# Prompt heads of a decoder step in pairs: scores from two row halves, values into two column halves

## The chip, the cores and the metric

The kernel runs on one core of a Trainium2 chip. A core has a matrix engine (TensorE, PE in the profile; PEld is its loading of weights), VectorE (DVE), ScalarE (ACT), GpSimd (POOL) and SyncE (SP), which work side by side and tell each other of progress through semaphores. Transfers between the chip's main memory and the on-chip memory are issued by SP and POOL and carried out by DMA engines. TensorE writes to PSUM, eight banks of 128 partitions x 512 floats, and VectorE and ScalarE read it from there. The metric is the time of one execution on the device in microseconds (us), lower is better.

## What is computed

One layer of a decoder for 256 prompt tokens and 64 sample tokens (8 sequences of 8), 2048 wide, all in float32: RMS norm, one projection whose columns are shared by three groups (a gated MLP, windowed attention with 16 heads of 64, cross-attention into 256 memory tokens with 4 heads of 128), an output projection, and a mixture of experts. The change concerns the windowed attention of the prompt:

```python
def dilated_attend_prompt(q, k, v, rel_bias):
    ...
    for window, dil in DILATIONS:
        ...
        sc = jnp.einsum("brnqhe,brnkhe->brnhqk", qs, kk) * scale + bias
        sc = jnp.where(valid[None, None, :, None], sc, -jnp.inf)
        m = jnp.max(sc, axis=-1, keepdims=True)
        p = jnp.exp(sc - m)
        l = jnp.sum(p, axis=-1, keepdims=True)
        o = jnp.einsum("brnhqk,brnkhe->brnqhe", p / l, vv)
        ...
    return combine_by_denominator(outs, lses).astype(dtype)
```

The three patterns, mixed by their softmax denominators, are one softmax per query over all keys, in which a key counts as often as patterns reach it. The kernel puts that count, as a logarithm, into the bias.

## The kernel before

The order of the work on each engine is written out by hand: all engines walk through the same 108 steps of the input projection. A step `s` does one unit on TensorE (`unit`): four 128-row slices of the model's width times 512 columns for one group of tokens. Units with `s % 3` of 0 and 1 have 128 tokens and fill the whole array (L499, 4 products). The third has the 64 sample tokens and puts two products of 256 columns into two column halves of the array (L502, 8 products). The weights come through a ring of four buffers that SP refills, four units of three steps ahead.

Attention is fitted between the units. Tables of step numbers say when:

- `START` holds the first step of each of eight sample units `n` (two sequences each). In steps 0 to 2 of a unit its keys are multiplied (`qk`, L613, L619), VectorE adds the bias (`soften`, L1139 to L1151), ScalarE takes the exponential (`sample_exp`, L930), in steps 3 to 5 the weights are transposed (`turn_s`, L629), in steps 4 to 6 they meet the values (`pv`, L646), and one step later the parts are folded (`fold`, L653).
- `HEAD_AT` holds one step for each of 16 prompt heads `h` (38 to 45, 74 to 81) and 4 memory heads (92 to 95). In that step TensorE makes the head's scores from the 64 rows of its half (`scores`, L556, L557, PSUM bank 3), VectorE adds the bias and takes the maximum (`head_max`, L1090 to L1097), and ScalarE the exponential (`head_exp`, L919, L920). One step later VectorE divides (`head_share`, L1103 to L1105), TensorE turns the three blocks of weights (`turn_p`, L570 to L572, bank 4) and ScalarE copies them back (`head_turned`, L926). Two steps later TensorE multiplies them with the values (`head_values`, L591, L592, bank 5, the 64 partitions of the head's half), and after each second head VectorE copies the pair out (`head_out`, L1112). The weights live in three buffers, `sc_p[h % 3]`.
- `NORM_AT` and `TURN_AT` place the norms of queries and keys on VectorE (`squares_of`, `normalise`, L1055 to L1077) and their transposes (L540, L542). Before each sample unit VectorE fills its padded query (`pad_q`, L1121).

Within a step TensorE does the unit first, then the scores, then sample work, then values and turns of heads.

Of the kernel before, what the change touches and what calls it, by code (L numbers as in the profile page):

```python
# [24 lines left out]
ALU = mybir.AluOpType  # L25
# [11 lines left out]
H, DH = 16, 64  # L37
HP = H // 2
G, DG = 4, 128
# [71 lines left out]
def hybrid_step(nc, x_rows, mem_rows, x_t, mem_t, w_proj, w_o, kc, vc, mkc, mvc, cst_d, gv_d, gffn_d,  # L111
                relb_d, onehot_d, w_gu, w_dn, mst_d, o_y, o_k, o_v, o_va, o_mk, o_mv,
                bias_d, bias_q_d):
    with ExitStack() as ctx:
# [374 lines left out]
        def _(pe):  # L489
# [55 lines left out]
            def scores(h):  # L545
                if h == 0:
                    pe.wait_ge(tr_used, 12)
                if h == 8:
                    pe.wait_ge(tr_used, 20)
                if h == H:  # L550
                    pe.wait_ge(tr_used, 24)
                if h:
                    pe.wait_ge(sc_read, h)
                if h < H:
                    r, hp = slice(64 * (h % 2), 64 * (h % 2) + 64), h % 8 // 2
                    mm(ps[:, 3, 0:128], qT[r, hp, 0:128], kT[r, hp, 0:128], start=True, stop=True)  # L556
                    mm(ps[:, 3, 128:384], qT[r, hp, 128:256], kT[r, hp, 0:256], start=True, stop=True).then_inc(sc_mm, 1)  # L557
                else:
                    g = h - H
                    mm(ps[:, 3, 0:256], qmT[:, g, 0:128], mkT[:, g, :], start=True, stop=True)  # L560
                    mm(ps[:, 3, 256:512], qmT[:, g, 128:256], mkT[:, g, :], start=True, stop=True).then_inc(sc_mm, 1)

            def turn_p(h):

                pe.wait_ge(p_ready, h + 1)
                if h:
                    pe.wait_ge(pt_ready, h)
                p = sc_p[h % 3]
                if h < H:
                    mm(ps[:, 4, 0:128], p[:, 0:128], c("flip"), start=True, stop=True)  # L570
                    mm(ps[:, 4, 128:256], p[:, 128:256], c("flip"), start=True, stop=True)
                    mm(ps[:, 4, 256:384], p[:, 256:384], c("flip"), start=True, stop=True).then_inc(pt_mm, 1)  # L572
                else:
                    tr(ps[:, 4, 0:128], p[:, 0:128], ident)
                    tr(ps[:, 4, 128:256], p[:, 256:384], ident)
                    tr(ps[:, 4, 256:384], p[:, 128:256], ident)
                    tr(ps[:, 4, 384:512], p[:, 384:512], ident).then_inc(pt_mm, 1)

            def head_values(h):
                pe.wait_ge(pt_ready, h + 1)  # L580
                pt = sc_p[h % 3]
                if h < H:
                    r = slice(64 * (h % 2), 64 * (h % 2) + 64)
                    if h == 0:
                        pe.wait_ge(z_ready, 4 + 9)
                    if h == 8:
                        pe.wait_ge(z_ready, 4 + 18)
                    if h % 2 == 0 and h >= 2:
                        pe.wait_ge(y_used, h // 2)
                    v = [z[:, Z_V[h // 8], t, (h % 8) * DH:(h % 8 + 1) * DH] for t in range(2)]  # L590
                    mm(ps[r, 5, 0:256], v[0], pt[:, 0:256], start=True, stop=False, skip_group_check=True)  # L591
                    mm(ps[r, 5, 128:256], v[1], pt[:, 256:384], start=False, stop=True, skip_group_check=True).then_inc(pv_mm, 1)  # L592
                else:
                    g = h - H
                    pe.wait_ge(y_used, HP + g)
                    mm(ps[:, 5, 0:256], mv[:, 0, g * DG:(g + 1) * DG], pt[:, 0:256], start=True, stop=False)
                    mm(ps[:, 5, 0:256], mv[:, 1, g * DG:(g + 1) * DG], pt[:, 256:512], start=False, stop=True).then_inc(pv_mm, 1)
# [115 lines left out]
            for s in range(UNITS_X):  # L713
# [154 lines left out]
        def _(act):  # L868
# [45 lines left out]
            def head_exp(h):  # L914
                act.wait_ge(mx_ready, h + 1)
                b, w0, w = h % 3, *((128, 384) if h < H else (256, 512))
# [97 lines left out]
        def _(dve):  # L1014
# [92 lines left out]
            def head_out(h):  # L1107
                if h < H and h % 2 == 0:
                    return
# [456 lines left out]
```

## Time and profile before

| | |
|---|---|
| median of 3 runs | 1237.83 us (1234.96 to 1239.39) |
| the profiled execution | 1238.09 us, span 1236.2 us |
| TensorE busy | 1125.1 us (91%) |
| VectorE, ScalarE, GpSimd busy | 349.5, 219.9, 39.9 us |
| mean share of the DMA engines | 76.1% for the main queue |
| the chain that ended last | TensorE 73%, DMA 19%, VectorE 3% |

The span is the time from the first to the last instruction. The chain is followed back from the last instruction, at each step to what released it. Projection and attention come first in the span, then the output projection, the routing and the loop over experts. A row of the timeline gives a start, a length, and in brackets how long the engine was idle before and for whom. Matmuls overlap at their ends, so what a group of them costs is read from its start to the start of the next.

### The profile page before, as it was taken

To read this page: it belongs to the slowest core of one execution; us is meant where nothing else is said; L and a number is where in the kernel's file an instruction comes from. 1 tells how busy PE (TensorE), PEld (TensorE's weight loads), DVE (VectorE), ACT (ScalarE), POOL (GpSimd) and SP (SyncE) were. 2 spreads that over 40 slices of the span, in tenths; PEclk is the share of its full clock that TensorE was granted. 3 is DMA by queue.
4 is the path that set the end of the run, shared out by engine and by line. 5 is a ranking of instruction groups with operands and counts; after the bars stand their busy time and mean duration, and the time that the engine had idled before them with its cause. 6 is when DMAs were issued, how large, how long until landed. Compare 5 with 4: busy or idle time off the path is not lost.

```text
span 1236.2 us, 15447 instructions
## 1 busy us (share of the span) xinstructions
PE 1125.1 (91%) x6547; PEld 480.1 (39%) x6547; DVE 349.5 (28%) x702; ACT 219.9 (18%) x434; POOL 39.9 (3%) x38
## 2 busy tenths in 40 slices
PE   6999999998999999999999995997979797979786
PEld 2344444553444554554444442232323232222222
DVE  2131112332211433250001114242424242333333
ACT  0400102220111221430001013121212211111120
POOL 0111010010010000010000000000000000000000
PEclk9999999999999999999999997998989898989899
DMA  7997246778999878752683213999999999999993
GB/s 246 361 354 302 103 142 261 276 302 324 380 337 366 337 284 317 318 217 102 256 344 118 85 34 137 426 433 429 432 424 432 430 434 428 435 429 426 435 426 142
DMA packets 33194, 385.20 MB, mean 312 GB/s; under 512 B 4207, under 2 KB 6383, under 8 KB 8655
## 3 DMA queue, kind: packets, MB, share of 16 engines
q1 hardware_dynamic: 31584, 378.96, 76.1%
q0 software_dynamic: 1568, 5.62, 1.5%
q8 instruction: 33, 0.54, 0.2%
q14 instruction: 9, 0.07, 0.0%
HBM read 376.67 MB, written 7.90 MB: 311 GB/s over the span
## 4 chain that ended last, share of the span: by engine, by line
PE 73%; DMA 19%; DVE 3%; ACT 2%; issue 2%; SPq 1%; POOL 1%; ACTq 0%; DVEq 0%; POOLq 0%
PE ps L499 27%; DMA arena<-w_gu 14%; PE ps L832 8%; PE ps L502 7%; PE ps L857 5%; PE ps L817 4%; PE ps L646 3%; DMA arena<-w_proj 3%; PE ps L613 3%; PE ps L844 3%; PE ps L837 1%; PE ps L862 1%; PE ps L629 1%; DMA arena<-x_rows 1%; PE ps L542 1%
## 5 line engine op out<-in xcount | busy, mean ns | idle before, releaser
L499 PE MATMUL ps<-arena 128*128 128x512 f32 x960 | 435.2, 602 | 12.5 <-DMA arena<-w_proj 12.5
L499 PEld LDWEIGHTS ps<-arena 128*128 128x128 f32 x960 | 176.7, 191 | 221.7 <-issue 220.1
L832 PE MATMUL ps<-arena 128*32 128x512 f32 x1024 | 133.0, 666 | 41.1 <-DMA arena<-w_gu 40.1
L817 PE MATMUL ps<-arena 128*32 128x512 f32 (+1 forms) x792 | 97.6, 606 | 6.5 <-DVE arena L1340 6.5
L502 PE MATMUL ps<-arena 128*64 128x256 f32 x832 | 101.3, 385 | 0.0
L832 PEld LDWEIGHTS ps<-arena 128*32 128x32 f32 x1024 | 35.8, 121 | 137.5 <-issue 122.4
L844 PE MATMUL ps<-arena 128*32 128x512 f32 x512 | 67.1, 645 | 20.6 <-DVE arena L1363 20.6
L1361 DVE STREAM_TRANSPOSE arena<-ps 128x512 f32<-128x512 f32 x32 | 22.9, 717 | 208.2 <-PE ps L817 208.2
L502 PEld LDWEIGHTS ps<-arena 128*64 128x64 f32 x832 | 55.1, 136 | 47.3 <-issue 23.5
L857 PE MATMUL ps<-arena 128*128 128x512 f32 x128 | 57.0, 598 | 9.5 <-ACT arena L1010 9.5
L1378 DVE COPY arena<-ps 32x512 f32<-32x512 f32 x64 | 44.2, 691 | 49.3 <-PE ps L844 48.3
L1003 ACT COPY arena<-ps 128x512 f32<-128x512 f32 x32 | 18.8, 586 | 205.4 <-PE ps L832 205.4
L817 PEld LDWEIGHTS ps<-arena 128*32 128x32 f32 (+1 forms) x792 | 23.0, 109 | 74.3 <-issue 74.3
L1008 ACT COPY arena<-ps 32x512 f32<-32x512 f32 x64 | 36.8, 575 | 82.1 <-PE ps L844 81.3
L1383 DVE TENSOR_TENSOR arena<-ps,arena 128x512 f32<-128x512 f32 x64 | 44.2, 691 | 21.3 <-PE ps L857 21.3
L1263 DVE TENSOR_TENSOR arena<-ps,arena 128x512 f32<-128x512 f32 (+1 forms) x16 | 8.9, 556 | 127.8 <-PE ps L499 122.9
L646 PE MATMUL ps<-arena 128*32 128x256 f32 (+1 forms) x704 | 44.0, 383 | 0.0
L1404 POOL TENSOR_TENSOR stat<-stat,nhalf 128x24 f32<-128x24 f32 (+4 forms) x9 | 25.0, 2781 | 564.5 <-DVE stat L1057 365.7
L613 PE MATMUL ps<-arena 128*32 128x512 f32 (+1 forms) x384 | 40.5, 540 | 2.9 <-issue 2.9
L837 PEld LDWEIGHTS ps<-arena 128*128 128x128 f32 x256 | 31.0, 191 | 26.8 <-issue 26.8
L857 PEld LDWEIGHTS ps<-arena 128*128 128x128 f32 x128 | 23.7, 190 | 37.3 <-issue 26.8
L898 ACT ACTIVATE arena<-ps,stat 128x512 f32<-128x512 f32 (+1 forms) x36 | 20.8, 578 | 95.7 <-PE ps L499 85.0
(226 smaller groups left out, 757.3 us busy)
## 6 DMA issues: line engine op xcount, KB each, us to landing
arena<-w_gu SPq DMA_DIRECT2D x32, 4096.0 KB, 21.8
arena<-w_dn SPq DMA_DIRECT2D x32, 2048.0 KB, 20.3
arena<-w_proj SPq DMA_DIRECT2D x44, 1024.0 KB, 7.3
arena<-kc SPq DMA_DIRECT2D x16, 2048.0 KB, 8.5
arena<-vc SPq DMA_DIRECT2D x16, 2048.0 KB, 8.6
arena<-w_o SPq DMA_DIRECT2D x16, 1024.0 KB, 4.8
arena<-kc SPq DMA_DIRECT2D x8, 1024.0 KB, 8.5
arena<-vc SPq DMA_DIRECT2D x8, 1024.0 KB, 9.0
```

The source lines that it names most:

```text
L499: last = mm(ps[:, bank + t, :], src[:, kt, r0:r0 + m], wring[:, i % QTR, k, :], start=start, stop=stop)
L502: last = mm(ps[64 * j:64 * j + 64, bank + t, 0:256], src[:, kt, r0:r0 + m], wring[:, i % QTR, k, 256 * j:256 * j + 256], start=start, stop ...
L613: last = mm(ps[32 * g:32 * g + 32, 6, 0:w], qpad[:, e * 128 + 32 * g:e * 128 + 32 * g + 32], kp[j][:, e, :], start=half == 0, stop=half == 1)
L646: last = mm(ps[32 * g:32 * g + 32, 7, 0:256], pt_s[0:w, t, 32 * g:32 * g + 32], v, start=t == 0, stop=t == VT)
L817: last = mm(ps[32 * j:32 * j + 32, 1, :], pm[0:m, t, 32 * s:32 * s + 32], n2[0:m, t, 512 * j:512 * j + 512], start=t == 0, stop=t == 2)
L832: last = mm(ps[g:g + 32, 0, :], xgT[:, r, kt, :], wgu[r][:, kt, :], start=kt < 4, stop=kt >= KT - 4)
L837: last = mm(ps[:, 2, 32 * f:32 * f + 32], part[:, 128 * f:128 * f + 128], sel, start=True, stop=True)
L844: last = mm(ps[32 * g:32 * g + 32, 3, :], actT[:, j, :], wdn[r][:, j, 512 * g:512 * g + 512], start=j == 0, stop=j == 1)
L857: mm(ps[:, 4 + n, :], pwT[:, t * P:(t + 1) * P], y4[:, 512 * n:512 * n + 512], start=True, stop=True).then_inc(comb_mm, 1)
L1008: copy(y4[32 * s:32 * s + 32, 512 * g:512 * g + 512], ps[32 * g:32 * g + 32, 3, :]).then_inc(ye_copied, 1)
L1378: V.tensor_copy(y4[32 * s:32 * s + 32, 512 * g:512 * g + 512], ps[32 * g:32 * g + 32, 3, :]).then_inc(ye_copied, 1)
L1383: V.tensor_tensor(hh, ps[:, 4 + n, :], hh, ALU.add).then_inc(added[t], 1)
```

## The change

The 16 prompt heads are handled as eight pairs, at the steps of `PAIR_AT`. A pair's scores are made in one go in the first step: the two heads lie in rows 0 to 63 and 64 to 127, their products alternate, and they go to banks 3 and 4. VectorE and ScalarE take maximum and exponential of both heads in that step and divide in the next. Two steps after the scores TensorE turns all six blocks, back into banks 3 and 4, and ScalarE copies both. Three steps after the scores, which is the step of the next pair's scores, the values of both heads are multiplied, alternating between the two column halves, into bank 5. Weights now live in `sc_p[0]` and `sc_p[1]`. Memory heads keep their functions, steps and order under new names.

```diff
-HEAD_AT = [38 + h for h in range(8)] + [74 + h for h in range(8)] + [92 + g for g in range(4)]
+PAIR_AT = (38, 41, 44, 47, 74, 77, 80, 83)
...
+def place(h):
+
+    return (h % 2, 128, 384) if h < H else ((h - H) % 3, 256, 512)
...
+            def pair_scores(p):
+
+                pe.wait_ge(tr_used, 12 if p < 4 else 20)
+                if p:
+                    pe.wait_ge(pt_ready, 2 * p)
+                hp = p % 4
+                lo, hi = slice(0, 64), slice(64, 128)
+                mm(ps[:, 3, 0:128], qT[lo, hp, 0:128], kT[lo, hp, 0:128], start=True, stop=True)
+                mm(ps[:, 4, 0:128], qT[hi, hp, 0:128], kT[hi, hp, 0:128], start=True, stop=True)
+                mm(ps[:, 3, 128:384], qT[lo, hp, 128:256], kT[lo, hp, 0:256], start=True, stop=True).then_inc(sc_mm, 1)
+                mm(ps[:, 4, 128:384], qT[hi, hp, 128:256], kT[hi, hp, 0:256], start=True, stop=True).then_inc(sc_mm, 1)
+
+            def pair_turn(p):
+
+                pe.wait_ge(sc_read, 2 * p + 2)
+                for k in range(2):
+                    pe.wait_ge(p_ready, 2 * p + k + 1)
+                    for a in range(0, 384, 128):
+                        last = mm(ps[:, 3 + k, a:a + 128], sc_p[k][:, a:a + 128], c("flip"), start=True, stop=True)
+                    last.then_inc(pt_mm, 1)
+
...
+            def pair_values(p):
+
+                pe.wait_ge(pt_ready, 2 * p + 2)
...
+                if p:
+                    pe.wait_ge(y_used, p)
+
+                def v(k, t):
+                    h = 2 * (p % 4) + k
+                    return z[:, Z_V[p // 4], t, h * DH:(h + 1) * DH]
+                lo, hi = slice(0, 64), slice(64, 128)
+                mm(ps[lo, 5, 0:256], v(0, 0), sc_p[0][:, 0:256], start=True, stop=False, skip_group_check=True)
+                mm(ps[hi, 5, 0:256], v(1, 0), sc_p[1][:, 0:256], start=True, stop=False, skip_group_check=True)
+                mm(ps[lo, 5, 128:256], v(0, 1), sc_p[0][:, 256:384], start=False, stop=True, skip_group_check=True)
+                mm(ps[hi, 5, 128:256], v(1, 1), sc_p[1][:, 256:384], start=False, stop=True, skip_group_check=True).then_inc(pv_mm, 1)
...
-                for h in range(H + G):
-                    if s == HEAD_AT[h]:
-                        scores(h)
+                for p, at in enumerate(PAIR_AT):
+                    if s == at + 3:
+                        pair_values(p)
+                for p, at in enumerate(PAIR_AT):
+                    if s == at:
+                        pair_scores(p)
...
-                for h in range(H + G):
-                    if s == HEAD_AT[h] + 2:
-                        head_values(h)
-                for h in range(H + G):
-                    if s == HEAD_AT[h] + 1:
-                        turn_p(h)
...
+                for p, at in enumerate(PAIR_AT):
+                    if s == at + 2:
+                        pair_turn(p)
...
             def head_turned(h):
                 w = 384 if h < H else 512
                 act.wait_ge(pt_mm, h + 1)
-                copy(sc_p[h % 3][:, 0:w], ps[:, 4, 0:w]).then_inc(pt_ready, 1)
+                copy(sc_p[place(h)[0]][:, 0:w], ps[:, 3 + h % 2 if h < H else 4, 0:w]).then_inc(pt_ready, 1)
...
-                for h in range(H + G):
-                    if s == HEAD_AT[h]:
-                        head_exp(h)
+                for p, at in enumerate(PAIR_AT):
+                    if s == at:
+                        head_exp(2 * p)
+                        head_exp(2 * p + 1)
...
-                for h in range(H + G):
-                    if s == HEAD_AT[h] + 1:
-                        head_turned(h)
+                for p, at in enumerate(PAIR_AT):
+                    if s == at + 2:
+                        head_turned(2 * p)
+                        head_turned(2 * p + 1)
...
-                    V.scalar_tensor_tensor(sc_p[b][:, 0:128], ps[:, 3, 0:128], S_WIN, bias[:, 128:256], ALU.mult, ALU.add)
-                    last = V.scalar_tensor_tensor(sc_p[b][:, 128:384], ps[:, 3, 128:384], S_WIN, bias, ALU.mult, ALU.add)
+                    V.scalar_tensor_tensor(sc_p[b][:, 0:128], ps[:, 3 + b, 0:128], S_WIN, bias[:, 128:256], ALU.mult, ALU.add)
+                    last = V.scalar_tensor_tensor(sc_p[b][:, 128:384], ps[:, 3 + b, 128:384], S_WIN, bias, ALU.mult, ALU.add)
...
-                for h in range(H + G):
-                    if s == HEAD_AT[h] + 1:
-                        head_share(h)
+                for p, at in enumerate(PAIR_AT):
+                    if s == at + 1:
+                        head_share(2 * p)
+                        head_share(2 * p + 1)
...
-                for h in range(H + G):
-                    if s == HEAD_AT[h]:
-                        head_max(h)
+                for p, at in enumerate(PAIR_AT):
+                    if s == at:
+                        head_max(2 * p)
+                        head_max(2 * p + 1)
...
-                for h in range(H + G):
-                    if s == HEAD_AT[h] + 2:
-                        head_out(h)
+                for p, at in enumerate(PAIR_AT):
+                    if s == at + 3:
+                        head_out(p)
```

On TensorE, in steps 40 and 41, before: L646 are sample values, L629 sample transposes, L591 and L592 a head's values, L570 to L572 its turns, L502 the third unit, L556 and L557 the next head's scores.

```order
L646 MATMUL ps<-arena 32x256 x16
L629 MATMUL ps<-cst,arena 128x128 x4
L591 MATMUL ps<-arena 64x256
L592 MATMUL ps<-arena 64x128
L570 MATMUL ps<-cst,arena 128x128
L571 MATMUL ps<-cst,arena 128x128
L572 MATMUL ps<-cst,arena 128x128
L502 MATMUL ps<-arena 64x256 x8
L556 MATMUL ps<-arena 128x128
L557 MATMUL ps<-arena 128x256
```

The same place now, where L663 are sample values, L646 sample transposes, L569 the six turns of pair 0, L508 the third unit, L584 to L587 the values of pair 0 and L558 to L561 the scores of pair 1:

```order
L663 MATMUL ps<-arena 32x256 x16
L646 MATMUL ps<-cst,arena 128x128 x4
L569 MATMUL ps<-cst,arena 128x128 x6
L508 MATMUL ps<-arena 64x256 x8
L584 MATMUL ps<-arena 64x256
L585 MATMUL ps<-arena 64x256
L586 MATMUL ps<-arena 64x128
L587 MATMUL ps<-arena 64x128
L558 MATMUL ps<-arena 128x128
L559 MATMUL ps<-arena 128x128
L560 MATMUL ps<-arena 128x256
L561 MATMUL ps<-arena 128x256
```

The turns stand next to the sample transposes, the values next to the third unit, which has their shape, and the scores of the next pair follow them.

On TensorE, in steps 49 and 50, before, there is no head work: L499 is the unit of step 49, L646 are the last sample values of unit 1, L502 is the unit of step 50, L613 the first sample scores of unit 2.

```order
L499 MATMUL ps<-arena 128x512 x4
L646 MATMUL ps<-arena 32x256 x12
L502 MATMUL ps<-arena 64x256 x8
L613 MATMUL ps<-arena 32x512 x8
L653 MATMUL ps<-cst,arena 128x32 x2
```

Now the turns (L569) and the values (L584 to L587) of pair 3 stand between these sample values (L663) and the sample scores (L630):

```order
L505 MATMUL ps<-arena 128x512 x4
L663 MATMUL ps<-arena 32x256 x12
L569 MATMUL ps<-cst,arena 128x128 x6
L508 MATMUL ps<-arena 64x256 x8
L584 MATMUL ps<-arena 64x256
L585 MATMUL ps<-arena 64x256
L586 MATMUL ps<-arena 64x128
L587 MATMUL ps<-arena 64x128
L630 MATMUL ps<-arena 32x512 x8
```

The work of the pair's end moved past the end of sample unit 1.

On VectorE, in step 38, before: a head's bias and maximum (L1090 to L1097) and then the last part of the scores of sample unit 0 (L1142, L1146) and its maximum (L1151).

```order
L1090 SCALAR_TENSOR_TENSOR arena<-ps,arena 128x128
L1091 SCALAR_TENSOR_TENSOR arena<-ps,arena 128x256
L1096 TENSOR_REDUCE stat<-arena 128x1
L1097 TENSOR_REDUCE stat<-arena 128x1
L1142 SCALAR_TENSOR_TENSOR arena<-ps,arena 128x256
L1146 SCALAR_TENSOR_TENSOR arena<-ps,arena 64x64 x2
L1151 TENSOR_REDUCE stat<-arena 128x1
```

Now the same for two heads (L1123 to L1130 twice) and then the sample unit (L1172, L1176, L1181):

```order
L1123 SCALAR_TENSOR_TENSOR arena<-ps,arena 128x128
L1124 SCALAR_TENSOR_TENSOR arena<-ps,arena 128x256
L1129 TENSOR_REDUCE stat<-arena 128x1
L1130 TENSOR_REDUCE stat<-arena 128x1
L1123 SCALAR_TENSOR_TENSOR arena<-ps,arena 128x128
L1124 SCALAR_TENSOR_TENSOR arena<-ps,arena 128x256
L1129 TENSOR_REDUCE stat<-arena 128x1
L1130 TENSOR_REDUCE stat<-arena 128x1
L1172 SCALAR_TENSOR_TENSOR arena<-ps,arena 128x256
L1176 SCALAR_TENSOR_TENSOR arena<-ps,arena 64x64 x2
L1181 TENSOR_REDUCE stat<-arena 128x1
```

The sample unit's part moved behind a second head's four operations.

## Rows read from the trace of the kernel before

**Rows 1.** Four stretches: length, busy PE, PEld, DVE, ACT, POOL (count), clock, DMA share, GB/s.

```profile
203.00:266.00 63.00, 63.00 (x451) 33.57 (x447) 23.70 (x76) 19.60 (x54) 0.00 (x0) 1.00 0.71 274
280.00:287.00 7.00, 5.14 (x23) 2.21 (x24) 2.73 (x8) 0.00 (x0) 0.00 (x0) 0.76 1.06 396
300.00:395.00 95.00, 93.94 (x661) 43.80 (x665) 17.30 (x34) 16.23 (x34) 6.75 (x5) 1.00 0.91 341
395.00:470.00 75.00, 74.50 (x487) 37.45 (x479) 29.45 (x86) 18.79 (x53) 0.00 (x0) 1.00 0.81 318
```

**Rows 2.** Waits of TensorE: for whom, us in total, times, longest.

```profile
PE ps L499 <- DMA arena<-w_proj: 12.5, 2, 10.2
...
PE ps L629 <- ACT arena L930: 3.5, 4, 2.2
PE ps L613 <- issue: 2.9, 1, 2.9
```

**Rows 3.** Timeline of TensorE around a head: start, length, line, shapes, count of passes.

```profile
210.23 0.39 PE L570 MATMUL ps<-cst,arena 128*128 128x128 f32 x2
...
210.90 3.60 PE L499 MATMUL ps<-arena 128*128 128x512 f32 x8
...
217.73 0.65 PE L591 MATMUL ps<-arena 128*64 128x256 f32 x2
...
218.52 0.49 PE L570 MATMUL ps<-cst,arena 128*128 128x128 f32 x2
...
219.39 1.95 PE L502 MATMUL ps<-arena 128*64 128x256 f32 x16
221.27 0.49 PE L556 MATMUL ps<-arena 64*128 64x128 f32 x2
...
222.12 1.07 PE L646 MATMUL ps<-arena 128*32 128x256 f32 x16
```

**Rows 4.** The chain that ended last, around 211 us: start, length, what.

```profile
211.06 3.44 PE ps L499 x8
```

**Rows 5.** Timeline of TensorE in step 50.

```profile
277.03 1.95 PE L502 MATMUL ps<-arena 128*64 128x256 f32 x16
281.86 3.09 PE L613 MATMUL ps<-arena 128*32 128x512 f32 x16 [2.89 <-issue]
```

**Rows 6.** Timeline of VectorE in step 50.

```profile
277.25 0.48 DVE L1160 SCALAR_TENSOR_TENSOR arena<-ps,stat,cst 128x256 f32<-128x256 f32 x1 [7.00 <-PE ps L646]
...
279.56 1.90 DVE L1077 TENSOR_TENSOR arena<-arena,gv 128x512 f32<-128x512 f32 x3
281.38 0.39 DVE L1121 COPY arena<-arena 64x64 f32<-64x64 f32 x2
```

**Rows 7.** Timeline of TensorE: three of the four waits before sample transposes.

```profile
300.24 0.66 PE L629 MATMUL ps<-cst,arena 128*128 128x128 f32 x4 [2.16 <-ACT arena L930]
...
334.57 0.66 PE L629 MATMUL ps<-cst,arena 128*128 128x128 f32 x4 [0.41 <-ACT arena L930]
...
465.09 0.66 PE L629 MATMUL ps<-cst,arena 128*128 128x128 f32 x4 [0.50 <-ACT arena L930]
```

**Rows 8.** Timeline of all engines in steps 38 to 41: a head's softmax and copy.

```profile
204.14 0.29 DVE L1090 SCALAR_TENSOR_TENSOR arena<-ps,arena 128x128 f32<-128x128 f32 x1 [2.01 <-PE ps L557]
...
205.39 0.43 DVE L1142 SCALAR_TENSOR_TENSOR arena<-ps,arena 128x256 f32<-128x256 f32 x1
205.44 0.40 ACT L919 ACTIVATE arena<-arena,stat 128x128 f32<-128x128 f32 x1 [14.04 <-DVE stat L1097]
...
206.24 0.19 ACT L920 ACTIVATION_READ_ACCUMULATOR arena<-arena,stat 128x1 f32 x1
...
207.69 0.15 DVE L1103 RECIPROCAL stat<-stat 128x2 f32<-128x2 f32 x1
...
208.08 0.35 DVE L1105 TENSOR_SCALAR arena<-arena,stat 128x256 f32<-128x256 f32 x1
...
219.50 0.48 ACT L926 COPY arena<-ps 128x384 f32<-128x384 f32 x1 [1.07 <-PE ps L572]
```

More of the change, by code:

```diff
@@ L563, in turn_p @@
[L563 to L597, printed above, removed]
+            def pair_scores(p):
[8 more added lines that the diff above has]
+                mm(ps[:, 4, 128:384], qT[hi, hp, 128:256], kT[hi, hp, 0:256], start=True, stop=True).then_inc(sc_mm, 1)
@@ new lines, in mhead_scores, with mhead_turn @@
+            def mhead_scores(g):
+                if g == 0:
+                    pe.wait_ge(tr_used, 24)
+                else:
+                    pe.wait_ge(sc_read, H + g)
+                mm(ps[:, 3, 0:256], qmT[:, g, 0:128], mkT[:, g, :], start=True, stop=True)
+                mm(ps[:, 3, 256:512], qmT[:, g, 128:256], mkT[:, g, :], start=True, stop=True).then_inc(sc_mm, 1)
+            def mhead_turn(g):
+                pe.wait_ge(p_ready, H + g + 1)
+                pe.wait_ge(pt_ready, H + g)
+                p = sc_p[g % 3]
+                tr(ps[:, 4, 0:128], p[:, 0:128], ident)
+                tr(ps[:, 4, 128:256], p[:, 256:384], ident)
+                tr(ps[:, 4, 256:384], p[:, 128:256], ident)
+                tr(ps[:, 4, 384:512], p[:, 384:512], ident).then_inc(pt_mm, 1)
@@ L599, in qk, with mhead_values @@
+            def mhead_values(g):
+                pe.wait_ge(pt_ready, H + g + 1)
+                pe.wait_ge(y_used, HP + g)
+                pt = sc_p[g % 3]
+                mm(ps[:, 5, 0:256], mv[:, 0, g * DG:(g + 1) * DG], pt[:, 0:256], start=True, stop=False)
+                mm(ps[:, 5, 0:256], mv[:, 1, g * DG:(g + 1) * DG], pt[:, 256:512], start=False, stop=True).then_inc(pv_mm, 1)
             def qk(n, j):
@@ L720, in _ @@
                 n, i = sample_step(s)
-                for h in range(H + G):
-                    if s == HEAD_AT[h]:
-                        scores(h)
+                for p, at in enumerate(PAIR_AT):
[4 more added lines that the diff above has]
+                        pair_scores(p)
+                for g, at in enumerate(MHEAD_AT):
+                    if s == at:
+                        mhead_scores(g)
                 if n is not None:
@@ L953, in _ @@
                     evict(s // 12, s % 3)
-                for h in range(H + G):
-                    if s == HEAD_AT[h]:
-                        head_exp(h)
+                for p, at in enumerate(PAIR_AT):
+                    if s == at:
+                        head_exp(2 * p)
+                        head_exp(2 * p + 1)
+                for g, at in enumerate(MHEAD_AT):
+                    if s == at:
+                        head_exp(H + g)
                 n, i = sample_step(s)
@@ L965, in _ @@
                     memory_copy((s - MEM_AT) // 2)
-                for h in range(H + G):
-                    if s == HEAD_AT[h] + 1:
-                        head_turned(h)
+                for p, at in enumerate(PAIR_AT):
+                    if s == at + 2:
+                        head_turned(2 * p)
+                        head_turned(2 * p + 1)
+                for g, at in enumerate(MHEAD_AT):
+                    if s == at + 1:
+                        head_turned(H + g)
                 for k, at in enumerate(TURN_AT):
@@ L1236, in _ @@
                     memory_out(1)
-                for h in range(H + G):
-                    if s == HEAD_AT[h] + 2:
-                        head_out(h)
+                for p, at in enumerate(PAIR_AT):
+                    if s == at + 3:
+                        head_out(p)
+                for g, at in enumerate(MHEAD_AT):
+                    if s == at + 2:
+                        head_out(HP + g)
                 for k, at in enumerate(NORM_AT):
```

48 lines of the change are left out of this document (22 added, 26 removed).

## The prediction

> **What bounds the kernel now.** I first cut the span into stretches to find who is busy where the heads are handled: in 203 to 266 us TensorE is busy for all 63.00 us, in 395 to 470 us for 74.50 of 75, and the DMA engines have a share of 0.71 and 0.81 there [rows 1]. Then the waits of TensorE: in the whole program there is none for keys or values, and in the steps of the prompt's attention, sample units included, only four for ScalarE (3.5 us together) and one for something unnamed (2.9 us); the 12.5 us for projection weights have no room in stretches as busy as these [rows 1, 2]. So a microsecond of TensorE work removed there is a microsecond of the span, and later stages, the expert loop too, start that much earlier, unless a new wait takes it. Third, the timeline of TensorE, read from start to start, because its matmuls overlap at their ends.
>
> **What a head costs TensorE.** Every product runs as two passes. Eight passes of 512 columns take 3.44 us in the chain [rows 4], 0.43 a pass, so a product of 128 columns streams in 0.215 us and one of 256 in 0.43. The scores of a head stream 0.645 us but take 0.85 (221.27 to 222.12), the values stream 0.645 and take 0.79 (217.73 to 218.52), the turns take 0.67 (210.23 to 210.90) where full-size work stands on both sides and 0.87 (218.52 to 219.39) where it is half-width work [rows 3]. So going into another shape of the array and out of the old one costs 0.20 us for the scores (64 rows), 0.145 for the values (64 columns) and 0.20 back to full size.
>
> **Column halves.** The third unit of a chunk quarter puts 16 passes of 256 columns through two column halves and takes 1.88 us (219.39 to 221.27) [rows 3]; 16 times 0.215 would be 3.44. Two column halves run at the same time. The new values of a pair alternate between these halves: both heads in 0.645 instead of twice that, 0.645 x 8 pairs = **5.2 us** saved.
>
> **Row halves.** No row of before has two row halves side by side, so I bound this. The lower bound is a head's scores as they are, one after the other: 0 saved. The upper is that the halves overlap as column halves do: again **5.2 us**. They go into two PSUM banks, need no other shape between them, and otherwise are built like the column pair; I take 5.2 and keep 0.
>
> **Fewer changes of shape.** I counted the runs of one shape over the whole TensorE order: full size 128 before and 120 after, 64 columns 74 and 61, 64 rows 46 and 38. The values lose more than 8 since all eight pairs follow a third unit, which already has their shape. 8 x 0.20 + 13 x 0.145 + 8 x 0.20 = **5.1 us** saved.
>
> **The wait at 279 us.** Step 50 waits 2.89 us before its sample scores [rows 5]. Of the engines that feed them, VectorE ends last: only when the sample values of step 49 are done (TensorE turns to the next unit at 277.03) can it mask them, then it normalises the queries of the second eight heads and fills the padded query, until 281.38 + 0.39 = 281.77 [rows 6]. That path of 4.83 us stays, for after puts no head work into it on VectorE. But the turns of pair 3 (6 x 0.223 + 0.20 = 1.54 us) and its values (0.645) now stand inside it, with the unit 1.54 + 1.88 + 0.645 = 4.06 us. The wait shrinks to about 0.8: **2.1 us** of head work is hidden. The clock comes with it: in 280 to 287 us the granted clock was 0.76 on average, 1.00 in the three stretches around [rows 1], that is, a part at 1.2 GHz directly after that idle time. 7 x 0.24 = **1.7 us**. Waits of 2.16, 0.41 and 0.50 us [rows 7] were not followed by such a fall, so I expect none after 0.8.
>
> **New waits.** The transposes of a sample unit wait for its softmax; with one full unit of TensorE between, that is 0.41 us (334.57) [rows 7]. Before, a head's scores stood in steps 39, 46 (there other head work) and 76 and covered it; after, nothing does: 3 x 0.41. In step 38 both maxima now stand ahead of the sample's last softening on VectorE; one head's takes 204.14 to 205.39 = 1.25 us [rows 8], so step 39 waits 1.7. In step 83 the pair's values and scores (1.5 us) cover the 0.50 that is there now [rows 7]. Sum: 1.7 + 0.4 + 0.4 - 0.5 = **2.0 us** lost.
>
> **What stays hidden.** The pair's own chain on VectorE and ScalarE: two maxima 2.5 us, the second exponential 1.0 (205.44 to 206.43), its share 0.74 (reciprocal at 207.69, last product until 208.43) [rows 8], with handovers some 4.5 us from the scores to the last weights. Between scores and turns lie two full units (3.44 us each at least [rows 4]) and sample work, 8 us at least. Then two copies of 0.48 us follow the turns [rows 8], the first while the second head is being turned, under the third unit's 1.88. Were that cover gone, a pair would pay about 1 us. The work of VectorE, ScalarE and the DMA queues is the same in number and size; SP's issues hang on TensorE's progress and move with it. SP's wait for the first eight heads' scores at step 48 stands behind its wait for the sample values of that step, which come later.
>
> **Sum.** 5.2 + 5.2 + 5.1 + 2.1 + 1.7 - 2.0 = 17.3 us. The profiled execution took 1238.09 us (span 1236.2); its run is 0.3 above the median of 1237.83. 1238.1 - 17.3 = 1220.8, say **1221 us**.
>
> **Rivals.** (1) *Row halves run one after the other*: 5.2 less, 1226 us. For it: nothing shows them together. Against it: the column halves. (2) *Passes start strictly in program order.* Both passes of one product stand before the first of the other half, so only one neighbouring pass of each overlaps: 0.107 + 0.107 + 3 x 0.215 = 0.86 for a pair's scores instead of 0.645, 0.215 x 8 = 1.7 us, 1222.7; for the values too, 1224.4. Against it for columns: in strict order the third unit would need 9 turns of 0.215, 1.94, and it takes 1.88 with its change of shape in it [rows 3]. By "TensorE: Matmul & The Clock Gate" of the Trainium skill, Part 3, The mechanism, matmuls start and end in strict order, only weight loads are pulled ahead; by that rule this rival is what happens, and the trace of the column halves disagrees. (3) *One more fall of the clock* after the 1.7 us wait of step 39 or the 2.2 of step 53: 1.7 us each, 1223 to 1224. (4) *Transfers become the bound*: the stretches with heads have shares of 0.71 and 0.81 [rows 1], so they could shrink by 19% at least before the DMA fills them, and 8 us of 63 is 13%; about 1236 if keys came late after all. (5) *Slower: the pair's softmax comes late.* Two heads arrive at once at VectorE, and if the 4.5 us stood open before the turns of every pair, 8 x 4.5 = 36 us would be lost: 1257. It decides from 2.2 us of open wait per pair on (17.3 / 8), that is, if the chain took over 10 us against its cover of 8; the rows add up to 4.5. "TensorEngine Tiling (Array Packing)" of the Trainium skill, PSUM Bottleneck, warns of just this: tiling speeds TensorE up, not the emptying of PSUM. Here VectorE is busy 23.7 us of 63 [rows 1], which speaks against it.
>
> **Chances and range.** Forecast 0.60; (1) 0.15, (2) 0.12, (3) 0.08, (4) 0.03, (5) 0.02. Repeats of before spread from 1234.96 to 1239.39, so a median may move by 2 us, and 0.3% (3.7 us) is about what a measurement can tell from no change. The range goes from 1217 (no wait left in steps 39 and 50, 2.5 us less, and 1.5 of that spread) to 1228 (rival 1 and 2 of the spread). Faster by over 0.3%: 0.95, within: 0.03, slower: 0.02.
>
> **What would show it.** Scores of a pair in 0.85 us from start to start, with both halves' passes starting together (1.5 says rival 1, 1.06 rival 2); values with the third unit in 2.5; step 50's wait under 1 us and the clock at 1.00 there; a wait of 1.7 us in step 39; the expert loop as before, begun some 17 us earlier. Wrong would be a wait in front of the turns or values of a pair, or for keys.

## The result and the profile after

The changed kernel takes 1223.12 us, median of 4 runs (1220.70 to 1224.78), against 1236.99 us of the kernel before on the same chip (1234.96 to 1239.39): a ratio of 0.9883, 95% interval 0.9865 to 0.9901. That is 13.9 us less, where 17.3 were forecast. The profiled execution took 1222.72 us with a span of 1220.9. The views in this part are of the changed kernel where nothing else is said. The median alone does not tell the forecast's mechanism from rivals 2 and 3, whose times were 1222.7 and 1223 to 1224; the profile and the experiments do.

Waits of TensorE, whole program, as in [rows 2]; the columns are for whom, us in total, times, longest:

```profile
PE ps L646 <- ACT arena L956: 5.3, 6, 2.2
...
PE ps L584 <- ACT arena L952: 1.4, 1, 1.4
...
PE ps L630 <- issue: 0.7, 1, 0.7
```

L646 are the transposes of the sample units, L584 is the first product of a pair's values, L630 the sample scores. The wait for nothing named went from 2.9 to 0.7 us, the sample transposes wait longer, 5.3 instead of 3.5, and a wait that was not forecast stands before the values of a pair.

Timeline of TensorE, to be read beside [rows 3, 5, 7]: step 39, then steps 40 and 41 with the values of pair 0 (L584 to L587) and the scores of pair 1 (L558 to L561), then steps 50, 53 and 83:

```profile
209.28 0.66 PE L646 MATMUL ps<-cst,arena 128*128 128x128 f32 x4 [1.50 <-ACT arena L956]
...
217.09 1.95 PE L508 MATMUL ps<-arena 128*64 128x256 f32 x16
218.87 0.38 PE L584 MATMUL ps<-arena 128*64 128x256 f32 x1
218.88 0.38 PE L585 MATMUL ps<-arena 128*64 128x256 f32 x1
...
219.62 0.37 PE L558 MATMUL ps<-arena 64*128 64x128 f32 x1
219.63 0.37 PE L559 MATMUL ps<-arena 64*128 64x128 f32 x1
...
220.48 1.93 PE L663 MATMUL ps<-arena 128*32 128x256 f32 x32
...
272.87 1.92 PE L630 MATMUL ps<-arena 128*32 128x512 f32 x16 [0.71 <-issue]
...
289.62 0.66 PE L646 MATMUL ps<-cst,arena 128*128 128x128 f32 x4 [2.16 <-ACT arena L956]
290.11 5.30 PE L505 MATMUL ps<-arena 128*128 128x512 f32 x8
...
446.99 0.43 PE L584 MATMUL ps<-arena 128*64 128x256 f32 x1 [1.37 <-ACT arena L952]
```

Both heads' scores now take 219.62 to 220.48, 0.86 us, as long as one head's before. The third unit and both heads' values take 217.09 to 219.62, 2.53 us. The two halves start within 0.01 us of each other. And the eight passes of a unit at 290.11 took 5.30 us where 3.60 is usual: this is the clock.

Stretches of the span, columns as in [rows 1]:

```profile
42.00:49.00 7.00, 7.00 (x13) 2.14 (x12) 2.62 (x4) 2.00 (x2) 0.52 (x1) 0.76 0.88 332
203.00:266.00 63.00, 61.09 (x470) 31.39 (x465) 26.36 (x79) 19.25 (x54) 3.10 (x1) 1.00 0.84 321
270.00:277.00 7.00, 6.29 (x47) 3.12 (x44) 3.93 (x10) 0.15 (x1) 0.00 (x0) 1.00 1.05 398
288.00:295.00 7.00, 5.38 (x12) 2.42 (x12) 0.18 (x2) 2.09 (x3) 0.00 (x0) 0.76 0.81 324
```

The granted clock stays at 1.00 around step 50, where it had fallen before, and falls behind the wait of step 53 instead, to 0.76 over 7 us, that is 1.7 us lost at 1.2 GHz. (The first row is another fall, long before the heads, to which the last section comes back.) The DMA engines' share in 203 to 266 us rose from 0.71 to 0.84: still below full.

To compare stages without what lies outside, I take the time from the start of the first sample scores (step 36) to the start of the router's first product. Before, on TensorE:

```profile
193.97 1.92 PE L613 MATMUL ps<-arena 128*32 128x512 f32 x16
...
749.08 1.06 PE L804 MATMUL ps<-arena,cst 128*128 128x32 f32 x4 [4.40 <-DVE arena L1308]
```

And after:

```profile
192.79 1.92 PE L630 MATMUL ps<-arena 128*32 128x512 f32 x16
...
733.84 1.06 PE L830 MATMUL ps<-arena,cst 128*128 128x32 f32 x4 [4.40 <-DVE arena L1349]
```

555.11 us before, 541.05 after: 14.06 less. The other 1.2 us by which this profiled execution is shorter lie ahead of step 36, in work that the change does not touch. There the second wait for projection weights ended 1.2 us earlier, first row after, second before:

```profile
74.22 2.81 PE L505 MATMUL ps<-arena 128*128 128x512 f32 x6 [0.26 <-DMA arena<-w_proj]
...
75.41 4.10 PE L499 MATMUL ps<-arena 128*128 128x512 f32 x9 [2.28 <-DMA arena<-w_proj]
```

That this is chance is not shown, since before was profiled once, but its profiled execution lies 1.1 us above its median of 1236.99, and the medians differ by 13.9, about what the stage gives. The expert loop behind is the same, 40 us of waits for its weights.

### The profile page after: what moved, and what is told of

Its sections match the earlier page's. It is cut to its first block, busy times and chain, and to the rows that moved or that the text cites. A ratio compares the mean times of both kernels' runs of the same rounds, so it can differ in the third digit from the quotient of the medians.

```text
span 1220.9 us, 15445 instructions
## 1 busy us (share of the span) xinstructions
PE 1111.4 (91%) x6547; PEld 473.2 (39%) x6547; DVE 347.6 (28%) x702; ACT 219.9 (18%) x434; POOL 39.8 (3%) x38
## 4 chain that ended last, share of the span: by engine, by line
PE 74%; DMA 16%; DVE 4%; ACT 2%; issue 2%; POOL 1%; ACTq 0%; SPq 0%; DVEq 0%; POOLq 0%
PE ps L505 30%; DMA arena<-w_gu 14%; PE ps L858 8%; PE ps L508 7%; PE ps L883 5%; PE ps L843 4%; PE ps L663 3%; PE ps L630 3%; PE ps L870 3%; DMA arena<-w_proj 2%; PE ps L863 1%; PE ps L888 1%; PE ps L646 1%; DVE stat L1181 1%; ACT arena L956 1%
## 5 line engine op out<-in xcount | busy, mean ns | idle before, releaser
L508 PE MATMUL ps<-arena 128*64 128x256 f32 x832 | 101.3, 385 | 0.0
L508 PEld LDWEIGHTS ps<-arena 128*64 128x64 f32 x832 | 55.1, 136 | 47.0 <-issue 22.9
L663 PE MATMUL ps<-arena 128*32 128x256 f32 (+1 forms) x704 | 44.0, 383 | 0.1
L630 PE MATMUL ps<-arena 128*32 128x512 f32 (+1 forms) x384 | 39.3, 527 | 0.7 <-issue 0.7
```

The lines of the kernel that those rows point to most:

```text
L508: last = mm(ps[64 * j:64 * j + 64, bank + t, 0:256], src[:, kt, r0:r0 + m], wring[:, i % QTR, k, 256 * j:256 * j + 256], start=start, stop ...
L630: last = mm(ps[32 * g:32 * g + 32, 6, 0:w], qpad[:, e * 128 + 32 * g:e * 128 + 32 * g + 32], kp[j][:, e, :], start=half == 0, stop=half == 1)
L663: last = mm(ps[32 * g:32 * g + 32, 7, 0:256], pt_s[0:w, t, 32 * g:32 * g + 32], v, start=t == 0, stop=t == VT)
```

## The experiments

All are variants of the changed kernel that do the same work in another order. They ran in two batches: scores_apart to copies_first beside a kernel before of 1237.89 us, the last three and after_again beside one of 1236.83. The table gives the medians and ranges, the ratio to the kernel before of the same batch with its interval, and from the profile the stage just defined. A fall of the clock inside it, behind a wait or just ahead of the router, costs 1.7 us (7 x 0.24) and comes and goes, so the last column leaves it out. (The longer fall that begins some 2 to 3 us ahead of the router's product is in every execution.)

| kernel | us (range) | ratio to before | stage, us | falls in it | stage less 1.7 each |
|---|---|---|---|---|---|
| before | 1236.99 (1234.96 to 1239.39) | 1 | 555.11 | 1 | 553.41 |
| changed | 1223.12 (1220.70 to 1224.78) | 0.9883 [0.9865, 0.9901] | 541.05 | 1 | 539.35 |
| after_again | 1222.11 (1220.63 to 1222.97) | 0.9871 [0.9854, 0.9889] | 541.05 | 1 | 539.35 |
| scores_apart | 1231.57 (1229.86 to 1232.77) | 0.9949 [0.9933, 0.9966] | 548.56 | 1 | 546.86 |
| halves_in_blocks | 1222.59 (1221.57 to 1223.05) | 0.9875 [0.9855, 0.9894] | 539.69 | 0 | 539.69 |
| pairs_early | 1224.70 (1224.47 to 1227.14) | 0.9899 [0.9877, 0.9921] | 540.69 | 0 | 540.69 |
| copies_first | 1221.51 (1221.14 to 1223.74) | 0.9873 [0.9851, 0.9894] | 539.45 | 1 | 537.75 |
| sample_first | 1221.41 (1220.29 to 1223.14) | 0.9867 [0.9849, 0.9884] | 539.97 | 1 | 538.27 |
| normalise_first | 1222.57 (1221.13 to 1223.95) | 0.9883 [0.9865, 0.9900] | 538.57 | 0 | 538.57 |
| all_four | 1215.90 (1215.54 to 1216.91) | 0.9828 [0.9814, 0.9843] | 533.71 | 0 | 533.71 |

From halves_in_blocks to normalise_first the medians lie within 3.3 us, no further apart than the changed kernel's own runs; there the stage in the profile decides. It is one execution each, but it repeats: the changed kernel, profiled twice, gave 541.05 both times.

### scores_apart: the second head's scores by themselves, later in the step

My theory says that the two row halves run at the same time; rival 1 says one after the other. Here they cannot overlap, since sample work stands between them.

```diff
             def pair_scores(p):
...
-                mm(ps[:, 4, 0:128], qT[hi, hp, 0:128], kT[hi, hp, 0:128], start=True, stop=True)
                 mm(ps[:, 3, 128:384], qT[lo, hp, 128:256], kT[lo, hp, 0:256], start=True, stop=True).then_inc(sc_mm, 1)
+
+            def second_scores(p):
+                hp = p % 4
+                hi = slice(64, 128)
+                mm(ps[:, 4, 0:128], qT[hi, hp, 0:128], kT[hi, hp, 0:128], start=True, stop=True)
                 mm(ps[:, 4, 128:384], qT[hi, hp, 128:256], kT[hi, hp, 0:256], start=True, stop=True).then_inc(sc_mm, 1)
...
+                for p, at in enumerate(PAIR_AT):
+                    if s == at:
+                        second_scores(p)
```

> The second head's scores of each pair stand at the end of the step, with sample work of another shape between them and the first head's. If the row halves overlap only because they stand side by side, each of the two groups takes 0.85 us and the eight pairs lose 8 x 0.85 = 6.8 us (5.2 of overlap, 1.6 of eight more changes of shape): about 1229.5 against 1222.7 of the changed kernel's profiled run. If the overlap is worth nothing and only the changes of shape count, 1.6 us: 1224.3. No new wait is expected, since the second head's maximum still has two steps.

Timeline of TensorE in its step 38, where L634 are sample scores:

```profile
202.31 0.48 PE L558 MATMUL ps<-arena 64*128 64x128 f32 x2
202.64 0.59 PE L559 MATMUL ps<-arena 64*128 64x256 f32 x2
203.16 1.07 PE L634 MATMUL ps<-arena 128*32 128x256 f32 x16
...
204.38 0.48 PE L564 MATMUL ps<-arena 64*128 64x128 f32 x2
204.71 0.59 PE L565 MATMUL ps<-arena 64*128 64x256 f32 x2
205.23 0.70 PE L505 MATMUL ps<-arena 128*128 128x512 f32 x1
```

Each head takes 0.85 us (202.31 to 203.16, 204.38 to 205.23), together 1.70 against the pair's 0.86. Eight times 0.84 is 6.7; the stage grew by 7.5, and the distance to the kernel before of the same batch shrank by 7.6 (13.9 to 6.3). So the overlap is real and worth about 7 us with the change of shape that it saves. Rival 1 falls. Of the 0.8 us beyond the 6.7, 0.6 come in pairs 1, 3 and 5: from one third unit to the next they grew by 1.04 us each, where the second group stands behind full-size sample transposes. Why those cost more is open; pair 7, which has such transposes between its two groups, grew by 0.84.

### halves_in_blocks: both products of one half ahead of the other's

In the changed kernel the halves alternate product by product. If TensorE started passes only in the order of the program (rival 2), this order would let only neighbouring passes of the two halves overlap.

```diff
                 mm(ps[:, 3, 0:128], qT[lo, hp, 0:128], kT[lo, hp, 0:128], start=True, stop=True)
-                mm(ps[:, 4, 0:128], qT[hi, hp, 0:128], kT[hi, hp, 0:128], start=True, stop=True)
                 mm(ps[:, 3, 128:384], qT[lo, hp, 128:256], kT[lo, hp, 0:256], start=True, stop=True).then_inc(sc_mm, 1)
+                mm(ps[:, 4, 0:128], qT[hi, hp, 0:128], kT[hi, hp, 0:128], start=True, stop=True)
                 mm(ps[:, 4, 128:384], qT[hi, hp, 128:256], kT[hi, hp, 0:256], start=True, stop=True).then_inc(sc_mm, 1)
```

The products of the values are reordered in the same way.

> Same products, but both products of the first half stand ahead of both of the second, for the scores and for the values. If each half of the array works through its own products independently, nothing changes: 0.86 us for a pair's scores, 2.53 for the unit with the values, about 1222.7. If passes start strictly in program order, the second half can overlap only with the first half's last pass: about 1.27 us for the scores and 0.42 more for the values too, 16 x 0.42 = 6.7 us, about 1229.

Timeline of its scores of pair 1; in the program L558 and L559 are the first head's products, L560 and L561 the second's:

```profile
219.91 0.37 PE L558 MATMUL ps<-arena 64*128 64x128 f32 x1
219.93 0.37 PE L560 MATMUL ps<-arena 64*128 64x128 f32 x1
...
220.24 0.38 PE L559 MATMUL ps<-arena 64*128 64x256 f32 x1
...
220.78 0.42 PE L663 MATMUL ps<-arena 128*32 128x256 f32 x4
```

L560 starts 0.02 us after L558 and 0.31 us ahead of L559, which stands before it in the program. The group takes 0.87 us, where program order would have taken 1.27; the stage grew by 0.3 us in all. Rival 2 falls: each half works through its own products. "TensorE: Matmul & The Clock Gate" of the Trainium skill, Part 3, The mechanism, says that matmuls keep the program's order in start and end; the starts in these rows disagree with it for two halves of the array.

### pairs_early: the first four pairs three steps earlier

This takes pair 3's turns and values out of step 50 and leaves the rest.

```diff
-PAIR_AT = (38, 41, 44, 47, 74, 77, 80, 83)
+PAIR_AT = (35, 38, 41, 44, 74, 77, 80, 83)
```

> The first four pairs stand three steps earlier (35, 38, 41, 44), so the turns and values of pair 3 end in step 47 and no longer stand in the wait of step 50. Theory: that wait is a fixed path on VectorE of 4.8 us behind the sample values of step 49, and the head work hid in it. Then the wait is 2.9 us again instead of 0.7, that is 2.2 us more, and the clock may fall behind it again (1.7 us): 1225 to 1226.6. Rival: the wait shrank because head work left VectorE in those steps; then it stays at 0.7 and the time at 1222.7.

Its waits of TensorE in 200 to 470 us, the line of step 50:

```profile
PE ps L630 <- issue: 2.9, 1, 2.9
```

And its clock behind that wait (which ends at 275.5) and behind the one of step 53:

```profile
274.00:279.00 5.00, 3.46 (x23) 1.62 (x24) 2.31 (x7) 0.00 (x0) 0.00 (x0) 1.00 1.02 404
290.00:297.00 7.00, 4.84 (x28) 2.26 (x30) 0.86 (x2) 2.10 (x3) 0.00 (x0) 1.00 0.88 327
```

The wait is back at 2.9 us, so the 2.2 us of step 50 were pair 3's work placed inside it. (The stage grew by 1.3 only, since pair 0's scores, 0.86 us, now lie ahead of it.) But the clock did not fall, though the wait was as long as in [rows 5], and that was not as my step on the clock had it.

### copies_first: ScalarE copies pair 6's weights ahead of a sample exponential

ScalarE in step 82 of the changed kernel (L956 is the exponential of sample unit 6, L952 the copies of a pair's turned weights):

```profile
444.68 1.42 ACT L956 ACTIVATE arena<-arena,stat 128x1344 f32<-128x1344 f32 x1 [2.98 <-DVE stat L1181]
...
446.10 0.84 ACT L952 COPY arena<-ps 128x384 f32<-128x384 f32 x2
```

Step 82 is the third step of sample unit 6 and the step in which pair 6 is turned. ScalarE's order has the exponential first, and that waits 2.98 us for VectorE's maximum; the copies, whose turns are long done, queue behind it, and TensorE waits for them with the values. The experiment turns the two round.

```diff
                 n, i = sample_step(s)
+                early = n is not None and i == 2
+                for p, at in enumerate(PAIR_AT):
+                    if early and s == at + 2:
+                        head_turned(2 * p)
+                        head_turned(2 * p + 1)
                 if n is not None and i == 2:
                     sample_exp(n)
...
-                    if s == at + 2:
+                    if not early and s == at + 2:
                         head_turned(2 * p)
                         head_turned(2 * p + 1)
```

> In step 82 ScalarE copies the turned weights of pair 6 before the exponential of sample unit 6 instead of after it. Theory: the 1.37 us wait before the values of pair 6 in step 83 is only this order on ScalarE; it goes to 0, the 0.14 us wait in step 84 may stay, and no wait for the sample exponential takes its place, since turns, unit, values and scores (4.9 us) cover its 4.1: about 1.4 us less, 1221.3. Rival: the sample softmax ends last in that step anyway; then as much waiting stands before the sample transposes of step 83 instead and the time stays at 1222.7.

ScalarE in the same step of this kernel:

```profile
442.83 0.48 ACT L952 COPY arena<-ps 128x384 f32<-128x384 f32 x1 [1.40 <-PE ps L569]
443.50 0.48 ACT L952 COPY arena<-ps 128x384 f32<-128x384 f32 x1 [0.19 <-PE ps L569]
444.41 1.42 ACT L956 ACTIVATE arena<-arena,stat 128x1344 f32<-128x1344 f32 x1 [0.43 <-DVE stat L1186]
```

And TensorE, the values and the sample transposes of step 83:

```profile
445.17 0.38 PE L584 MATMUL ps<-arena 128*64 128x256 f32 x1
...
446.78 0.66 PE L646 MATMUL ps<-cst,arena 128*128 128x128 f32 x4
```

The wait is gone, none takes its place, and the sample transposes don't wait either. The stage is 1.6 us shorter, all of it in step 83; the 0.13 us that step 84 loses stay.

### sample_first and normalise_first: the order on VectorE in steps 38 and 49

In step 38 sample unit 0 goes ahead of the pair on VectorE. This is VectorE's part; ScalarE's order has the same edit for the exponential:

```diff
...
+                first = n is not None and i == 2 and s in PAIR_AT
+                if first:
+                    soften(n, i)
                 for p, at in enumerate(PAIR_AT):
                     if s == at:
                         head_max(2 * p)
...
-                if n is not None and i <= 2:
+                if n is not None and i <= 2 and not first:
                     soften(n, i)
```

> Base: the changed kernel, 1223.1 us. In step 38 VectorE softens sample unit 0 and ScalarE takes its exponential ahead of the pair's maxima and exponentials. If the 1.50 us wait of step 39 (209.28 us of the changed kernel) is owed to the order of these two engines, it falls to 0.4 to 0.5 us and the time to about 1222.0. If the pair's own softmax is then late for its turns in step 40, a wait of about the same size appears there and the time stays at 1223. If the waits of PE there are hidden by something behind it, nothing changes at all.

In step 49 the queries of the second eight heads are normalised ahead of the mask of sample unit 1:

```diff
+                if s == NORM_AT[3] + 1:
+                    normalise(3)
                 if n is not None and i == 6:
                     sample_mask(n)
...
-                    if s == at + 1:
+                    if s == at + 1 and k != 3:
                         normalise(k)
```

> Base: the changed kernel, 1223.1 us. In step 49 VectorE normalises sample unit 3 ahead of the mask of unit 1, so that the turns of step 50 find their input 0.8 us earlier. If the 0.71 us wait ahead of the turns of step 50 is VectorE's order, it goes and the time is about 1222.4. If it only moves to step 51, whose mask is then late, the time stays at 1223.1.

VectorE of the changed kernel in steps 49 and 50, which answers to [rows 6]:

```profile
268.25 0.48 DVE L1190 SCALAR_TENSOR_TENSOR arena<-ps,stat,cst 128x256 f32<-128x256 f32 x1 [5.43 <-PE ps L663]
268.65 1.89 DVE L1103 TENSOR_TENSOR arena<-arena,stat 128x512 f32<-128x512 f32 x3
270.57 1.90 DVE L1111 TENSOR_TENSOR arena<-arena,gv 128x512 f32<-128x512 f32 x3
272.38 0.39 DVE L1151 COPY arena<-arena 64x64 f32<-64x64 f32 x2
```

The norms (L1103, L1111) stand behind a mask that waits 5.43 us for TensorE. With them in front:

```profile
266.98 1.90 DVE L1103 TENSOR_TENSOR arena<-arena,stat 128x512 f32<-128x512 f32 x3 [4.31 <-POOL stat L1447]
...
270.72 0.48 DVE L1190 SCALAR_TENSOR_TENSOR arena<-ps,stat,cst 128x256 f32<-128x256 f32 x1
...
```

In normalise_first TensorE's wait in step 50 is gone and the stage is 0.8 us shorter. In sample_first the wait of step 39 is 0.41 us, as TensorE's timeline of it shows, and the stage is 1.1 us shorter:

```profile
208.70 0.66 PE L646 MATMUL ps<-cst,arena 128*128 128x128 f32 x4 [0.41 <-ACT arena L956]
```

The medians of sample_first and normalise_first moved by -0.7 us and +0.5 us against the changed kernel in the same batch (after_again), within the ranges, so the size of these two is told by the profile alone.

### all_four: the three orders, and the last pair of the first half at steps 50 to 53

Besides the three edits above, pair 3 goes three steps back, so that its turns and values lie in steps 52 and 53, in front of the 2.16 us wait. The bias of the last four heads goes into the buffer that pairs 2 and 3 read, so it is loaded six steps later.

```diff
-PAIR_AT = (38, 41, 44, 47, 74, 77, 80, 83)
+PAIR_AT = (38, 41, 44, 50, 74, 77, 80, 83)
...
-                if s == 48:
-                    for quad in (2, 3):
+                for quad, at in ((2, 48), (3, 54)):
+                    if s == at:
                         sp.wait_ge(sc_read, 4 * (quad - 1))
                         window_bias(quad)
```

> The three changes of order together (step 82: copies ahead of the exponential, 1.37 us; step 38: sample unit 0 first, 1.1 us; step 49: normalise first, 0.7 us) and the last pair's scores at step 50 instead of 47, so that its turns and values lie in steps 52 and 53 and cover the 2.16 us wait of step 53. If these waits are all on the path and add up, 1.4 + 1.1 + 0.7 + 2.1 = 5.3 us are gone: about 1217.8 against 1223.1, and up to 1.7 us less where the clock fell behind the wait of step 53. If the waits only shift to the next step in each case, 1221 to 1223.

Its waits of TensorE, the one line left in this stage of those shown above, and its timeline in step 53:

```profile
PE ps L646 <- ACT arena L956: 2.0, 5, 0.4
```

```profile
284.60 0.38 PE L584 MATMUL ps<-arena 128*64 128x256 f32 x1
...
285.40 0.66 PE L646 MATMUL ps<-cst,arena 128*128 128x128 f32 x4
285.89 3.60 PE L505 MATMUL ps<-arena 128*128 128x512 f32 x8
```

1215.90 us: 1.7% under the kernel before, and 6.2 us under the changed kernel in the same batch (their ranges don't touch). The stage is 5.6 us shorter: 1.6 + 1.1 + 0.8 of the three orders and 2.2 of step 53 make 5.7. The waits were on the path and add up. But the last of the four did not run by itself, and it leans on normalise_first: pairs_early shows that step 50 waits 2.89 us again when pair 3's work leaves it. Here it does not, because on VectorE the norms are over before the sample values of step 49 are, and only the mask (L1199) and the filling of the padded query follow those:

```profile
263.14 1.90 DVE L1120 TENSOR_TENSOR arena<-arena,gv 128x512 f32<-128x512 f32 x3
266.13 0.48 DVE L1199 SCALAR_TENSOR_TENSOR arena<-ps,stat,cst 128x256 f32<-128x256 f32 x1 [1.10 <-PE ps L663]
```

The edit of copies_first also holds in step 52 here, the third step of sample unit 2.

### after_again: the changed kernel once more

> The changed kernel once more, beside the three others on one chip: 1223.1 us (1220.7 to 1224.8). The waits should stand where they stood (1.50 in step 39, 0.71 in step 50, 2.16 in step 53, 1.37 in step 83). Where the clock's fall behind the wait of step 53 belongs to the order of the work, it is there again; where it is chance, it may be missing, and the span of the profiled execution is then about 1.7 us shorter.

Two stretches of this second profiled execution, to be held against those of the first:

```profile
42.00:49.00 7.00, 7.00 (x17) 2.30 (x17) 2.78 (x5) 2.69 (x3) 0.52 (x1) 1.00 0.91 341
288.00:295.00 7.00, 5.07 (x32) 2.51 (x36) 0.50 (x2) 2.09 (x3) 0.00 (x0) 1.00 0.90 376
```

The waits are the same to 0.01 us, the weight wait ahead of the stage aside, but the clock did not fall behind step 53. It fell once elsewhere, just ahead of the router (0.72 over 724 to 730 us), so that the stage came out equal.

## Why the prediction was right, and where it was off

The direction, the mechanism and the main terms held, and the time lies in the range; 17.3 us were forecast and 15.4 came in the profiled pair of executions, 14.1 of them in the stage. By the prediction's own terms:

- **Column halves, row halves and fewer changes of shape**, 15.5 together, held. The pair's scores were to take 0.85 us and took 0.86, unit and values 2.53 against 0.645 + 1.88. What remains of the 14.06 when the measured waits are taken out is 14.06 - 2.18 + 3.55 = 15.4. That is a remainder for the three terms together; of them only the row halves were tried by themselves. These, for which there had been no row, run together like the column halves (scores_apart), and not in strict program order (halves_in_blocks).
- **The wait of step 50** was to shrink to 0.8 and shrank to 0.71; pairs_early shows that it is pair 3's work that fills it.
- **The clock behind it, 1.7**, is the first step that failed. The fall at step 50 did go, but another came at step 53, rival 3. More than that: I took a wait's length to decide, 2.89 falls and 2.16 does not. The runs don't bear that out. The wait of 2.16 us before step 53's transposes is in nine of the ten executions profiled; three of the nine fell there and six did not, the same kernel once so and once so. Of the two with 2.89 us in step 50, one fell. Behind the 0.7 us that the change leaves in step 50 none of six fell, so a chance of a fall may have gone there; but the term was no sure gain of the change. It was a chance of 1.7 us on either side, and in this pair of profiles it came to nothing. "TensorE: Matmul & The Clock Gate" of the Trainium skill, Part 1, What's actually happening, says that the window in which activity is judged runs freely and does not start with the kernel. That two executions of one kernel fell at different places fits that; no run here shows it further.
- **New waits, 2.0 lost**: steps 39, 46 and 76 came as forecast (1.50 for 1.7, and 0.41 twice), and the 0.50 of step 83's transposes went. The second failed step is here and in **what stays hidden**: I held the copies of a pair to be under the third unit's 1.88 us for all eight pairs. For pair 6 they stand behind a sample exponential on ScalarE that itself waits for VectorE, and step 83 lost 1.4 us before the values (1.6 in the stage, by copies_first); 0.13 us more stand before the sample values of step 84. I had looked at how long the copies take, not at what ScalarE has to do ahead of them in the one step where a pair's turns meet the third step of a sample unit. By the forecast's own sign ("a wait in front of the turns or values of a pair") this is where it was wrong. Together the waits cost 1.50 + 0.41 + 0.41 - 0.50 + 1.6 + 0.13 = 3.55 us.
- **What lay outside the sum**: 1.2 us of the profiled difference came ahead of step 36 from a weight wait, in work that the change does not touch.

So 17.3 - 1.7 (clock) - 1.6 (step 83) + 0.2 (step 39) - 0.1 gives the 14.1 of the stage. Rival 4 did not come: TensorE waits for no keys or values anywhere in the changed kernel, at a DMA share of 0.84. Of rival 5 there came one late pair of eight, through ScalarE's order in step 82 (1.6 us) and not through the pair's own softmax; ScalarE has time enough (19.25 us busy in 63). "TensorEngine Tiling (Array Packing)" of the Trainium skill, PSUM Bottleneck, warns that the emptying of PSUM may become the limit when tiling makes TensorE faster. What was late here was a copy out of PSUM, but for its place in a queue and not for the speed of copying.

## What to carry to other kernels

Where two heads use half of the array's rows or columns each, one group for both costs about what one head did, or less (0.86 against 0.85 us for the scores, 0.65 against 0.79 for the values), and the order of the products within the group hardly matters (0.87 for 0.86 us). Once TensorE is the bound, what such a change really yields depends also on what other engines have queued ahead of its small steps: walk through each engine's order at every place where two periodic works meet, here pairs of three steps with sample units of seven, before calling a copy hidden. Work that is free in its place is best put where TensorE still waits, once it is known what the place that it leaves will wait for: three changes of order and one such move in all_four gave another 6 us for no work saved.

## What was not expected of the hardware

- Two row halves take up their own products independently: a product started 0.31 us ahead of one of the other half that precedes it in the program (halves_in_blocks).
- The granted clock after the same wait differs from execution to execution: behind 2.16 us it fell in 3 of 9, and each fall cost 1.7 us. The three executions that fell there had also fallen between 44 and 49 us (0.76 over 42 to 49 us, as above), the other six had not; what ties the two together was not tried.
- The fall at 44 to 49 us came without a wait: TensorE was busy for all 7.00 us of that stretch. Ahead of it, from 39.98 to 44.54, it ran ten passes that use 33 rows and 16 columns of the array. The same ten stand in every execution profiled, and four of the ten executions fell behind them (these three and all_four).
